# The first unit's product on split rows without the norm's factor, the factor applied to its results

## The chip, the cores and the metric

The kernel runs on one core of one Trainium2 chip. The metric is the device time of one execution in microseconds (us); a median over several executions is compared. Below, PE is the matrix engine, PEld its weight loads, DVE the vector engine, ACT the scalar engine, POOL the general engine and SP the engine whose queue issues most DMAs.

## What is computed

One layer of a decoder for 512 prompt tokens and 8 sample tokens, held together as 520 columns. Only the start of the layer matters here:

```python
h = rmsnorm(x, g_mix_pre)      # x * g * (1 / sqrt(mean(x*x) + eps)), per token
proj = h @ w_in                # 2048 -> q | k | v | B | C | u | gate_a | gate_b
...
merged = sigmoid(ga + b_gate[0]) * branch_a + sigmoid(gb + b_gate[1]) * branch_b
x = x + rmsnorm(merged @ w_o, g_mix_post)
# then the ConvFFN (up, causal conv, gelu, down) and the per-layer embedding
```

The norm's factor belongs to a token, that is, to a column of the kernel's matrices. So (x * g) @ w times the factor per column equals h @ w: the factor can be applied to the result.

## The kernel before

**Layout and units.** Activations lie feature-major: 16 rows of 128 features (k = 0 to 15) by 520 tokens, each token range cut into two halves of 260 (HALF). The weights come from memory as a stream of quarters `s_raw` (128x1024, four for each unit, two sets of buffers) which SP's queue loads. A unit produces two tiles of 128 output features for all tokens. Units 0 to 31 are the input projection; 0 and 1 are gates. Most units use a Strassen-like scheme of seven half-size products (j = 0 to 6) on sums and differences of weight quarters (`s1` to `s4`, on DVE) and of row blocks (`t1` to `t4`, on DVE, made once for all units of a set). A set's first unit is *plain* in three sets (`PLAIN`): all 16 rows times both tiles, without sums, so that the row blocks can be prepared meanwhile.

**Precision.** A product is either in fp32 (line 994 for the plain unit, line 1028 for the second unit, line 829 for k and v), or it is split: `v_hi`/`v_lo` are the high and low part of a weight tile, `o_hi`/`lo` those of a row block, and three cheaper fp32r matmuls (high by high, low by high, high by low) stand for one fp32 matmul (line 1063; line 1153 in the branches). High parts are ACT copies (`v_high`, `o_high`), low parts are DVE subtractions (`v_low`, `o_low`). `v_hi` and `v_lo` have four slots each.

**The start.** ACT scales each row of x into `raw4` (`x_tile`, line 1211) and squares it (1215), DVE adds the squares (1697), PE multiplies k's and v's weights with the rows that have no factor yet (829) and sums the squares over the features by `square_sum` (812). ACT takes the root (1195), DVE the reciprocal (1683), and `h_row` multiplies all 16 rows in place by the factor (1703). PE's plain unit 0 follows (994): 16 rows by two tiles by two halves, 64 fp32 matmuls, each shown in the trace as two records.

**Who waits for whom.** Every engine works through a queue written out in program order; semaphores join them. ACT copies the four results of unit 0 to `d_h` (`plain_unit`, line 1318, semaphores c11_out to c21_out) and the first three results of unit 1 (`copied`, line 1271: r1_out, r5_out, r2_out) so that PE may write their banks again: unit 1 begins after c11_out, its product j = 2 after r1_out, its product j = 4 after r2_out (`banks_free`). DVE's order is set by `plain_unit`, `second_unit` and `unit`. From unit 2 on PE needs `v_lo` and the low parts of the row blocks.

Of the kernel before, what the change touches and what calls it, by code (L numbers as in the profile page):

```python
# [90 lines left out]
def build(nc, sstream, x_in, p_in, chan_in, sinkp_in, sinks_in, cstate_in, fstate_in,  # L91
# [5 lines left out]
    with ExitStack() as ctx:  # L97
# [33 lines left out]
        x_raw = at("x_raw", [P, KD, T], r_op)  # L131

# [205 lines left out]
        SPLIT = split_of(range(U_O))  # L338
# [103 lines left out]
        x_rdy = sem("x_rdy")  # L442
        kv_used = sem("kv_used")
# [19 lines left out]
        ss_ready = sem("ss_ready")  # L463
        ss_scaled = sem("ss_scaled")
        ss_shift = sem("ss_shift")
        ss_exp = sem("ss_exp")
        ss_prob = sem("ss_prob")
        ss_turned = sem("ss_turned")
        ss_copied = sem("ss_copied")
        ss_out = sem("ss_out")  # L470
# [330 lines left out]
        def _(pe):  # L801
# [38 lines left out]
            def sample_scores():  # L840
# [4 lines left out]
                for g in range(NKV):  # L845
# [5 lines left out]
                    mm.then_inc(ss_ready, 1)  # L851

            def sample_turn():
                pe.wait_ge(ss_prob, 1)
# [3 lines left out]
                mm.then_inc(ss_turned, 1)  # L858

            def sample_values():  # L860
                pe.wait_ge(ss_copied, 1)
# [6 lines left out]
                mm.then_inc(ss_out, 1)  # L868
# [132 lines left out]

            def raw_product(s, u, j, parity):
# [7 lines left out]
                for h in range(2):  # L1010
# [117 lines left out]
            first_unit(0)  # L1128
# [57 lines left out]
        def _(act):  # L1186
# [1583 lines left out]
```

## Time and profile before

| | |
|---|---|
| median of 3 runs | 2680.53 us (2680.52 to 2681.27) |
| the profiled execution | 2679.39 us |
| its span in the profile | 2677.6 us |
| PE busy | 2663.8 us, 99% of the span |
| DVE busy | 2172.0 us, 81% |
| ACT busy | 1341.0 us, 50% |

The span is what the profile covers; the time of that execution is 1.8 us more. Times below count from the span's start. A busy share is an average over stages with different limits, so the start has to be read in its own rows.

### The profile page before, as it was taken

What the parts mean: (1) busy time and instruction counts of PE and PEld (TensorE: products, weight loads), DVE (VectorE), ACT (ScalarE), POOL (GpSimd) and SP (SyncE); (2) the same over time, 40 slices, a digit from 0 to 9 for tenths busy, and PEclk for the clock granted to TensorE, in tenths of its full rate; (3) what the DMA queues carried; (4) which work ended last, traced back from release to release, by engine and by line L of the source; (5) the groups of instructions that cost most, each with busy time, mean ns of one, the idle gap of its engine ahead of it and who ended that gap; (6) DMA issues with size and microseconds to landing.
All of it is one profiled execution on the core that took longest, in us unless ns stands there. A gap on an engine that the chain in (4) does not pass through costs nothing.

```text
span 2677.6 us, 54973 instructions
## 1 busy us (share of the span) xinstructions
PE 2663.8 (99%) x20917; PEld 2599.2 (97%) x20917; DVE 2172.0 (81%) x3809; ACT 1341.0 (50%) x2429; POOL 162.6 (6%) x251
## 2 busy tenths in 40 slices
PE   9999999999999999999999999999999999999999
PEld 8999999999999999989999999999999999999899
DVE  5998888888843687898888888888888768789987
ACT  5444555555532255645555555555555453445354
POOL 0110000000000000000000000000000000000000
PEclk9999999999999999999999999999999999999999
DMA  6443333333443355655566555665568575565684
GB/s 222 134 145 130 125 117 119 131 131 123 160 158 140 132 152 166 232 184 159 159 200 201 167 178 165 185 196 178 157 191 291 166 250 160 160 207 168 230 267 144
DMA packets 151348, 460.55 MB, mean 172 GB/s; under 512 B 16442, under 2 KB 46914, under 8 KB 147809
## 3 DMA queue, kind: packets, MB, share of 16 engines
q1 hardware_dynamic: 125040, 367.55, 38.8%
q0 software_dynamic: 26000, 90.86, 15.2%
q8 instruction: 80, 1.31, 0.2%
q14 instruction: 84, 0.68, 0.1%
q10 hardware_dynamic: 144, 0.15, 0.0%
HBM read 403.24 MB, written 54.11 MB: 171 GB/s over the span
## 4 chain that ended last, share of the span: by engine, by line
PE 98%; DVE 1%; issue 0%; ACT 0%; DVEq 0%; POOL 0%; ACTq 0%; POOLq 0%
PE pair L1063 77%; PE pair L1153 7%; PE pair L1028 7%; PE pair L994 3%; PE pair L829 1%; PE pair L1123 1%; PE pair L881 1%; PE pair L902 1%; DVE v_lo L1909 0%; PE pair L891 0%; PE pair L1180 0%; PE pair L960 0%; DVE lo L2007 0%; PE pair L818 0%; DVE lo_A L2007 0%
## 5 line engine op out<-in xcount | busy, mean ns | idle before, releaser
L1063 PE MATMUL pair<-o_hi,v_hi 128*128 128x260 f32 x5778 | 1638.0, 283 | 1.6 <-DVE f_low L2455 0.9
L1063 PE MATMUL pair<-o_hi,v_lo 128*128 128x260 f32 x5778 | 1631.4, 282 | 0.0
L1238 ACT ACTIVATE v_hi<-s_raw 128x512 fp32r<-128x512 f32 (+1 forms) x1328 | 828.9, 627 | 1007.3 <-PE pair L1063 810.5
L1063 PE MATMUL pair<-lo,v_hi 128*128 128x260 f32 x4140 | 1169.5, 282 | 0.0
L1909 DVE TENSOR_TENSOR v_lo<-s_raw,v_hi 128x512 fp32r<-128x512 f32 (+1 forms) x1264 | 859.2, 682 | 303.0 <-ACT v_hi L1238 267.1
L1063 PEld LDWEIGHTS pair<-o_hi,v_hi 128*128 128x128 f32 x5778 | 1086.4, 188 | 13.7 <-issue 12.0
L1063 PEld LDWEIGHTS pair<-o_hi,v_lo 128*128 128x128 f32 x5778 | 1088.2, 188 | 0.0
L1063 PEld LDWEIGHTS pair<-lo,v_hi 128*128 128x128 f32 x4140 | 778.1, 188 | 0.3
L1063 PE MATMUL pair<-lo_E,v_hi 128*128 128x260 f32 x834 | 236.0, 283 | 0.0
L1063 PE MATMUL pair<-lo_A,v_hi 128*128 128x260 f32 x804 | 226.7, 282 | 0.0
L1238 ACT ACTIVATE v_hi<-s_one 128x512 fp32r<-128x512 f32 (+1 forms) x212 | 132.2, 627 | 178.3 <-PE pair L1063 153.1
L1951 DVE TENSOR_TENSOR s_raw<-s_one,s_raw 128x512 f32<-128x512 f32 (+1 forms) x226 | 152.1, 676 | 15.4 <-PE pair L1028 15.4
L1063 PEld LDWEIGHTS pair<-lo_E,v_hi 128*128 128x128 f32 x834 | 156.4, 188 | 0.0
L1960 DVE TENSOR_TENSOR s_raw<-s_raw,s_raw 128x512 f32<-128x512 f32 (+1 forms) x226 | 152.3, 675 | 0.0
L1941 DVE TENSOR_TENSOR s_raw<-s_raw,s_raw 128x512 f32<-128x512 f32 (+1 forms) x226 | 151.3, 675 | 0.0
L1063 PEld LDWEIGHTS pair<-lo_A,v_hi 128*128 128x128 f32 x804 | 151.1, 188 | 0.0
L1909 DVE TENSOR_TENSOR v_lo<-s_one,v_hi 128x512 fp32r<-128x512 f32 (+1 forms) x212 | 143.4, 678 | 5.2 <-ACT v_hi L1238 1.5
L1028 PE MATMUL pair<-raw,s_raw 128*128 128x260 f32 x628 | 141.3, 383 | 2.7 <-DVE g_half L2185 1.7
L1028 PEld LDWEIGHTS pair<-raw,s_raw 128*128 128x128 f32 x628 | 118.4, 190 | 21.8 <-DVE g_half L2185 2.1
L2629 POOL DMA_DIRECT2D s_one<-in_sstream x81 | 44.5, 550 | 1377.0 <-DVE s_raw L1951 1042.2
L1153 PE MATMUL pair<-br_hi,v_lo 128*128 128x260 f32 x512 | 103.2, 283 | 0.0
L1153 PE MATMUL pair<-br_lo,v_hi 128*128 128x260 f32 x512 | 103.0, 283 | 0.0
(232 smaller groups left out, 2324.3 us busy)
## 6 DMA issues: line engine op xcount, KB each, us to landing
s_raw<-in_sstream SPq DMA_DIRECT2D x468, 512.0 KB, 4.6
s_one<-in_sstream POOLq DMA_DIRECT2D x146, 512.0 KB, 5.3
raw<-f_scr SPq DMA_DIRECT2D x12, 1040.0 KB, 7.1
s_raw<-in_sstream SPq DMA_DIRECT2D x32, 384.0 KB, 4.1
g_scr<-d_h SPq DMA_DIRECT2D x16, 520.0 KB, 2.7
g_in<-g_scr SPq DMA_DIRECT2D x32, 260.0 KB, 2.7
x_scr<-y_sb SPq DMA_DIRECT2D x8, 1040.0 KB, 5.1
s_one<-in_sstream POOLq DMA_DIRECT2D x16, 384.0 KB, 4.6
```

Of the source, the lines that this page charges most:

```text
L829: mm = pe.matmul(pair[2 + n][:, h, 0:HALF], w[:, quarter_of(k)[2]], x_half(k, h), start=k == 0, stop=k == KD - 1, skip_group_check=True)
L881: mm = pe.matmul(bank[g][:, v * 256 + key:(v + 1) * 256], q_blk[n % 2][HD * g:HD * g + HD, v, :], kT_sb[HD * g:HD * g + HD, blk * BLK + ke ...
L994: mm = pe.matmul(pair[a][:, b, 0:HALF], s_raw[r % 2][q][:, k % KH * P:(k % KH + 1) * P], src, start=k == 0, stop=k == nk * 2 - 1, skip_gro ...
L1028: mm = pe.matmul(out, w[:, kk * P:kk * P + P], src[:, k, :], start=j in (0, 1, 3) and k == 0, stop=k == nk - 1, skip_group_check=True)
L1063: mm = pe.matmul(out, wt[:, slot, kk * P:kk * P + P], r[:, k, :], start=j in (0, 1, 3) and k == 0 and n == 0, stop=k == nk - 1 and n == 2, ...
L1153: mm = pe.matmul(pair[2 + p][:, half, 0:HALF], wt[:, slot, kk * P:kk * P + P], r[:, half * HALF:(half + 1) * HALF], start=k == 0 and i == ...
L1238: nc.scalar.activation(v_hi[:, n % 4, 0:width], src, ACT.Copy, scale=0.5 if u == "br" else 1.0).then_inc(v_hi_rdy, 1)
L1909: ins = dve.tensor_tensor(v_lo[:, n % 4, 0:width], src, high, ALU.subtract)
L1941: dve.tensor_tensor(quarter(u, 2, h), quarter(u, 0, h), quarter(u, 2, h), ALU.subtract)\
L1951: dve.tensor_tensor(quarter(u, 0, h), w_src(u, 1, h), quarter(u, 0, h), ALU.subtract)\
L1960: dve.tensor_tensor(quarter(u, 1, h), quarter(u, 1, h), quarter(u, 0, h), ALU.subtract)\
L2629: pool.dma_start(s_one[:, 0:n], sstream[r_of(u), 2, :, 0:n]).then_inc(s1_dma, 16)
```

## The change

Unit 0 is no longer made in fp32. `split_plain_unit` (PE) multiplies high and low parts of the rows *without* the factor (`x_hi`, `x_lo`) with high and low parts of unit 0's weights: 192 fp32r matmuls in the place of 64 fp32 ones. ACT makes 16 `x_high` and 8 more `v_high`, DVE 16 `x_low` and 8 more `v_low`. The factor is multiplied into unit 0's two results `d_h` by DVE in unit 1 (`h_evac`, `g_first`). `h_row` stays, for all later units, and now waits for `x_lo` of its row. `square_sum` moves behind two more rows of k and v. Since `x_lo` and `x_hi` lie where the row blocks' parts will lie, `o_high` and `t2`, `t3`, `t4` wait for rows of unit 0 to be used; `t3` and `t4` move from ahead of unit 1 into it. Some semaphores of the sample's attention are merged. The first ACT table is that of Sqrt, and the load of it before the root goes.

```diff
+        x_lo = at("x_lo", [P, KD, T], r_op, f32r)
+        x_hi = at("x_hi", [P, KD, T], r_op + 4 * HB, f32r)
...
-        SPLIT = split_of(range(U_O))
+        SPLIT = [("first", i, 0) for i in range(8)] + split_of(range(U_O))
...
+        def rows_used(k):
+
+            return k - 1
...
+            if u == "first":
+                return rows_used(4 * (j // 2) + 3) - 1
...
+            if u == "first":
+                r, q = r_of(0), 2 * (j % 2) + j // 4
+                return r, q, s_raw[r % 2][q][:, (j // 2 % 2) * 4 * P:(j // 2 % 2 + 1) * 4 * P]
...
-                if k == KD - 4:
+                if k == KD - 2:
...
+            def split_plain_unit():
+
+                pe.wait_ge(root_rdy, 1)
+                for k in range(KD):
+                    if k % 4 == 0:
+                        pe.wait_ge(v_lo_rdy, k // 2 + 2)
+                    pe.wait_ge(x_lo_rdy, k + 1)
+                    for wt, r in ((v_hi, x_hi), (v_lo, x_hi), (v_hi, x_lo)):
+                        for n, outs in enumerate((((0, 1), (1, 1)), ((0, 0), (1, 0)))):
+                            slot = (k // 4 * 2 + n) % 4
+                            for h in range(2):
+                                a, b = outs[h]
+                                mm = pe.matmul(pair[a][:, b, 0:HALF],
+                                               wt[:, slot, k % 4 * P:k % 4 * P + P],
+                                               r[:, k, h * HALF:(h + 1) * HALF],
+                                               start=k == 0 and wt is v_hi and r is x_hi,
+                                               stop=k == KD - 1 and r is x_lo, skip_group_check=True)
+                    if k >= 2:
+                        mm.then_inc(v_used, 1)
+
...
+                    elif s == 0 and j in (0, 3, 5):
+                        pe.wait_ge(h_rdy, KD if j else KH)
...
-            first_unit(0)
+            split_plain_unit()
...
-            nc.scalar.activation(table_out[:, 6:7], ones[:, 0:1], ACT.Square)
+            nc.scalar.activation(table_out[:, 6:7], ones[:, 0:1], ACT.Sqrt)
+
+            def x_high(k):
+
+                act.wait_ge(x_rdy, k + 1)
+                nc.scalar.activation(x_hi[:, k, :].rearrange("p (h t) -> p h t", h=2), x_tile(k), ACT.Copy)\
+                  .then_inc(x_hi_rdy, 1)
...
+                    if 5 <= k < 13:
+                        x_high(k - 5)
+            v_high(0)
+            v_high(1)
             root(0)
+            for k in range(8, 12):
+                x_high(k)
+            v_high(2)
+            v_high(3)
+            for k in range(12, KD):
+                x_high(k)
             bias = chan[:, C_BGATE:C_BGATE + 2 * KD]
             nc.scalar.activation(bias, bias, ACT.Copy, scale=0.5).then_inc(bias_half, 1)
             warm(ACT.Exp, 1)
...
+                if s == 0 and j < 5:
+                    act.wait_ge(v_used, rows_used((3, 7, 11, 15, 3)[j]))
...
-                early = 1 if s == 2 else 5
+                early = {0: 3, 2: 1, S_GATE: 5}[s]
+                if s == 0:
+                    v_high(4)
+                    v_high(5)
                 for j in range(early):
                     o_high(s, j)
+                    if s == 0 and j == 0:
+                        v_high(6)
+                        v_high(7)
...
+                if u == 0:
+                    act.wait_ge(g_first, n + 1)
...
+            def x_low(k):
+
+                dve.wait_ge(x_hi_rdy, k + 1)
+                dve.wait_ge(sq_ready, k + 1)
+                dve.tensor_tensor(two(x_lo[:, k, :]), x_tile(k), two(x_hi[:, k, :].bitcast(f32)), ALU.subtract)\
+                   .then_inc(x_lo_rdy, 1)
...
+                if 6 <= k < 14:
+                    x_low(k - 6)
+            v_low(0)
+            v_low(1)
             invert(1)
...
+                dve.wait_ge(x_lo_rdy, k + 1)
...
+            def first_free(s, j):
+
+                if s == 0:
+                    dve.wait_ge(v_used, rows_used({2: 7, 4: 11, 6: 15}[j]))
+
...
-                if s in (0, 2):
+                if s == 2:
...
+                if s == 0:
+                    both_halves(s1, u + 1)
+                    both_halves(t2, s)
+                    both_halves(s3, u + 1)
+                    return
...
+                    if i == 1 and s == 0:
+                        both_halves(t3, s)
+                    if i == 4 and s == 0:
+                        both_halves(t4, s)
...
+                if u == 1 and i == 2:
+                    for n in range(2):
+                        for e in ((c11_out, c12_out), (c22_out, c21_out))[n]:
+                            dve.wait_ge(e, 1)
+                        dve.tensor_tensor(d_h[0][:, n, :], d_h[0][:, n, :], rstd[:, :], ALU.mult)\
+                           .then_inc(g_first, 1)
...
+            v_low(2)
+            v_low(3)
             st.wait()
-            for k in range(KD):
+            for k in range(KH):
+                h_row(k)
+            for k in range(KH, KH + 4):
+                x_low(k)
+            v_low(4)
+            v_low(5)
+            dve.wait_ge(h_rdy, KH)
+            both_halves(t1, 0)
+            for k in range(KH + 4, KD):
+                x_low(k)
+            v_low(6)
+            v_low(7)
+            for k in range(KH, KD):
                 h_row(k)
             dve.wait_ge(h_rdy, KD)
...
+            pool.wait_ge(g_first, 2)
```

**DVE from the reciprocal to t2.** `raw_60` is the rows, `s_one` and `s_raw` weights, `raw_E` what t2 makes. Before:

```order
L1683 RECIPROCAL rstd<-rstd 128x520 [waits root_rdy]
L1703 TENSOR_TENSOR raw_60<-raw_60,rstd 128x2x260 [waits kv_used,dve_step]
L1703 TENSOR_TENSOR raw_60<-raw_60,rstd 128x2x260 [waits kv_used] x15
L1933 TENSOR_TENSOR s_one<-s_raw_51,s_raw_52 128x512 [waits s_rdy03,s_rdy02,h_rdy]
L1933 TENSOR_TENSOR s_one<-s_raw_51,s_raw_52 128x512 [waits s_rdy03,s_rdy02]
L1941 TENSOR_TENSOR s_raw_51<-s_raw_49,s_raw_51 128x512 [waits s_rdy00] x2
L1971 TENSOR_TENSOR raw_60<-raw_60 128x1040 [waits v_used] x2
L1979 TENSOR_TENSOR raw_E<-raw_60 128x1040 [waits t1_done] x2
```

The same place in the changed kernel, right after the reciprocal, two `v_lo` and the first eight row multiplications:

```order
L1767 TENSOR_TENSOR x_lo<-raw_60,x_hi 128x520 [waits sq_ready,x_hi_rdy] x4
L1760 TENSOR_TENSOR v_lo<-s_raw_54,v_hi 128x512 [waits v_hi_rdy]
L1760 TENSOR_TENSOR v_lo<-s_raw_56,v_hi 128x512 [waits v_hi_rdy]
L2045 TENSOR_TENSOR raw_60<-raw_60 128x1040 [waits h_rdy]
L2045 TENSOR_TENSOR raw_60<-raw_60 128x1040
L1767 TENSOR_TENSOR x_lo<-raw_60,x_hi 128x520 [waits sq_ready,x_hi_rdy] x4
L1760 TENSOR_TENSOR v_lo<-s_raw_54,v_hi 128x512 [waits v_hi_rdy]
L1760 TENSOR_TENSOR v_lo<-s_raw_56,v_hi 128x512 [waits v_hi_rdy]
L1787 TENSOR_TENSOR raw_60<-raw_60,rstd 128x2x260 [waits kv_used,x_lo_rdy] x8
L2002 TENSOR_TENSOR s_one<-s_raw_51,s_raw_52 128x512 [waits s_rdy03,s_rdy02,h_rdy]
L2002 TENSOR_TENSOR s_one<-s_raw_51,s_raw_52 128x512 [waits s_rdy03,s_rdy02]
L2054 TENSOR_TENSOR raw_E<-raw_60 128x1040 [waits t1_done,v_used]
```

Eight `x_lo`, four `v_lo` and all sixteen row multiplications now stand ahead of `raw_E` (t2); t1 comes between them.

**DVE in unit 1.** `raw_79` is t3's block, `raw_80` t4's, the `lo` rows are the low parts for unit 2. Before, t3 and t4 precede the first row shown:

```order
L1951 TENSOR_TENSOR s_raw_49<-s_one,s_raw_49 128x512 [waits s1_done,v_used] x2
L2007 TENSOR_TENSOR lo_69<-raw_60,o_hi_62 128x1040 [waits o_hi_rdy,v_used] x2
L1933 TENSOR_TENSOR s_one<-s_raw_55,s_raw_56 128x512 [waits v_used,s2_done,s_rdy13,s_rdy12] x2
L2007 TENSOR_TENSOR lo_70<-raw_60,o_hi_63 128x1040 [waits o_hi_rdy,v_used] x2
L2007 TENSOR_TENSOR lo_E<-raw_E,o_hi_64 128x1040 [waits o_hi_rdy,v_used] x2
L1960 TENSOR_TENSOR s_raw_50<-s_raw_50,s_raw_49 128x512 [waits s2_done,v_used,s_rdy01]
```

In the changed kernel:

```order
L2020 TENSOR_TENSOR s_raw_49<-s_one,s_raw_49 128x512 [waits s1_done,v_used] x2
L2063 TENSOR_TENSOR raw_79<-raw_E,raw_60 128x1040 [waits t2_done,v_used]
L2063 TENSOR_TENSOR raw_79<-raw_E,raw_60 128x1040 [waits t2_done]
L2084 TENSOR_TENSOR lo_71<-raw_60,o_hi_64 128x1040 [waits o_hi_rdy,v_used] x2
L2347 TENSOR_TENSOR d_h_103<-d_h_103,rstd 128x520 [waits c12_out,c11_out]
L2347 TENSOR_TENSOR d_h_103<-d_h_103,rstd 128x520 [waits c21_out,c22_out]
L2002 TENSOR_TENSOR s_one<-s_raw_55,s_raw_56 128x512 [waits v_used,s2_done,s_rdy13,s_rdy12] x2
L2084 TENSOR_TENSOR lo_72<-raw_60,o_hi_65 128x1040 [waits o_hi_rdy,v_used] x2
L2071 TENSOR_TENSOR raw_80<-raw_60,raw_E 128x1040 [waits v_used]
L2071 TENSOR_TENSOR raw_80<-raw_60,raw_E 128x1040
L2084 TENSOR_TENSOR lo_E<-raw_E,o_hi_66 128x1040 [waits o_hi_rdy,v_used] x2
L2029 TENSOR_TENSOR s_raw_50<-s_raw_50,s_raw_49 128x512 [waits s2_done,v_used,s_rdy01]
```

t3, the two multiplications of `d_h` by `rstd`, and t4 have moved or come into the stretch that runs while PE makes unit 1.

**ACT around unit 0's results.** `o_hi_..` are the high parts of the row blocks, L1318 the four copies of unit 0's results, L1271 those of unit 1. Before:

```order
L1265 ACTIVATE o_hi_64<-raw_E 128x1040 [waits t2_done] x2
L1265 ACTIVATE o_hi_65<-raw_60 128x1040 [waits h_rdy] x2
L1265 ACTIVATE o_hi_66<-raw_77 128x1040 [waits t3_done] x2
L1318 ACTIVATE d_h_101<-pair 128x260 [waits v_used]
L1318 ACTIVATE d_h_101<-pair 128x260 x3
L1271 ACTIVATE d_h_102<-pair 128x260 [waits v_used]
L1265 ACTIVATE o_hi_67<-raw_60 128x1040 [waits h_rdy] x2
L1271 ACTIVATE d_h_102<-pair 128x260 [waits v_used]
L1265 ACTIVATE o_hi_68<-raw_78 128x1040 [waits t4_done] x2
L1271 ACTIVATE d_h_102<-pair 128x260 [waits v_used]
```

In the changed kernel these are L1314, L1373 and L1320:

```order
L1314 ACTIVATE o_hi_66<-raw_E 128x1040 [waits t2_done]
L1373 ACTIVATE d_h_103<-pair 128x260 [waits v_used]
L1373 ACTIVATE d_h_103<-pair 128x260 x3
L1314 ACTIVATE o_hi_67<-raw_60 128x1040 [waits h_rdy,v_used]
L1314 ACTIVATE o_hi_67<-raw_60 128x1040 [waits h_rdy]
L1314 ACTIVATE o_hi_68<-raw_79 128x1040 [waits t3_done,v_used]
L1314 ACTIVATE o_hi_68<-raw_79 128x1040 [waits t3_done]
L1320 ACTIVATE d_h_104<-pair 128x260 [waits v_used]
L1314 ACTIVATE o_hi_69<-raw_60 128x1040 [waits h_rdy] x2
L1320 ACTIVATE d_h_104<-pair 128x260 [waits v_used]
L1314 ACTIVATE o_hi_70<-raw_80 128x1040 [waits t4_done] x2
L1320 ACTIVATE d_h_104<-pair 128x260 [waits v_used]
```

The four copies still stand behind the high part of `raw_E`; the copy that is r1_out now stands behind the high parts of t3's block, and r2_out behind those of t4's block.

## Rows read from the trace of the kernel before

**Rows 1.** The page: busy time, share of the span, instructions; the chain.

```profile
PE 2663.8 (99%) x20917; PEld 2599.2 (97%) x20917; DVE 2172.0 (81%) x3809; ACT 1341.0 (50%) x2429; POOL 162.6 (6%) x251
...
PE 98%; DVE 1%; issue 0%; ACT 0%; DVEq 0%; POOL 0%; ACTq 0%; POOLq 0%
```

**Rows 2.** Timeline of PE: start us, duration us, engine, line, names, count.

```profile
0.99 4.21 PE L818 MATMUL pair<-ones 128*128 128x128 f32 x18 [0.99 <-POOL table_out L2560]
5.12 22.22 PE L829 MATMUL pair<-raw,s_raw 128*128 128x260 f32 x96
27.18 1.04 PE L812 MATMUL pair<-sqacc,ones 128*128 128x260 f32 x4
28.05 7.18 PE L829 MATMUL pair<-raw,s_raw 128*128 128x260 f32 x32
35.07 28.22 PE L994 MATMUL pair<-raw,s_raw 128*128 128x260 f32 x128
```

**Rows 3.** Timeline of PE, units 1 and 2.

```profile
63.76 3.77 PE L1028 MATMUL pair<-raw,s_raw 128*128 128x260 f32 x16 [0.48 <-ACT d_h L1318]
...
88.22 0.47 PE L1063 MATMUL pair<-o_hi,v_hi 128*128 128x260 f32 x1
```

**Rows 4.** One line's records: duration min/median/max ns, first and last start.

```profile
L1153 PE MATMUL pair<-br_hi,v_hi x512: 278/282/288, 743.1 to 927.0; 128*128 128x260 f32 x171
...
L1153 PE MATMUL pair<-br_hi,v_lo x512: 277/283/291, 743.6 to 927.5; 128*128 128x260 f32 x171
```

**Rows 5.** Who PE waited for, whole span: us in total, times, longest.

```profile
PE pair L1028 <- DVE g_half L2185: 1.7, 1, 1.7
...
PE pair L1028 <- ACT d_h L1318: 0.5, 1, 0.5
```

**Rows 6.** Timeline of ACT.

```profile
24.27 0.64 ACT L1215 ACTIVATE sq_a<-x_raw 128x520 f32<-128x520 f32 x1
...
28.25 0.69 ACT L1195 ACTIVATE rstd<-pair,table_out 128x520 f32<-128x520 f32 x1 [1.83 <-PE pair L812]
...
51.72 2.22 ACT L1265 ACTIVATE o_hi<-raw_E 128x1040 fp32r<-128x1040 f32 x2
...
63.32 1.23 ACT L1318 ACTIVATE d_h<-pair 128x260 f32<-128x260 f32 x4 [5.53 <-PE pair L994]
...
71.08 0.39 ACT L1271 ACTIVATE d_h<-pair 128x260 f32<-128x260 f32 x1 [1.20 <-PE pair L1028]
```

**Rows 7.** Timeline of ACT, weights of unit 2.

```profile
76.11 1.14 ACT L1238 ACTIVATE v_hi<-s_raw 128x512 fp32r<-128x512 f32 x2
```

**Rows 8.** Timeline of DVE.

```profile
28.98 3.40 DVE L1683 RECIPROCAL rstd<-rstd 128x520 f32<-128x520 f32 x1 [3.34 <-ACT rstd L1195]
32.42 9.86 DVE L1703 TENSOR_TENSOR raw<-raw,rstd 128x520 f32<-128x520 f32 x16
42.31 1.29 DVE L1933 TENSOR_TENSOR s_one<-s_raw,s_raw 128x512 f32<-128x512 f32 x2
...
50.45 2.39 DVE L1979 TENSOR_TENSOR raw_E<-raw 128x1040 f32<-128x1040 f32 x2
...
65.82 0.69 DVE L1951 TENSOR_TENSOR s_raw<-s_one,s_raw 128x512 f32<-128x512 f32 x1 [8.37 <-PE pair L1028]
```

**Rows 9.** Timeline of DVE, unit 1.

```profile
74.16 2.38 DVE L2007 TENSOR_TENSOR lo_E<-raw_E,o_hi 128x1040 fp32r<-128x1040 f32 x2
...
78.09 0.43 DVE L2181 TENSOR_TENSOR d_h<-pair,d_h 128x260 f32<-128x260 f32 x1 [0.94 <-PE pair L1028]
...
88.43 0.68 DVE L1909 TENSOR_TENSOR v_lo<-s_raw,v_hi 128x512 fp32r<-128x512 f32 x1
```

**Rows 10.** Groups of PE in 7.5 to 9.2 us: count, busy us, mean ns.

```profile
L829 PE MATMUL pair<-raw,s_raw 128*128 128x260 f32 x9 | 2.1, 383 | 0.0
```

**Rows 11.** Groups of PE in 5 to 6.2 us.

```profile
L829 PE MATMUL pair<-raw,s_raw 128*128 128x260 f32 x3 | 1.7, 695 | 0.0
```

**Rows 12.** Records of line 1028: duration min/median/max ns.

```profile
L1028 PE MATMUL pair<-raw,s_raw x628: 380/382/487, 63.8 to 2550.3; 128*128 128x260 f32 x157
```

More of the change, by code:

```diff
@@ L442, in build @@
         x_rdy = sem("x_rdy")
+        x_hi_rdy = sem("x_hi_rdy")
+        x_lo_rdy = sem("x_lo_rdy")
+        g_first = sem("g_first")
         kv_used = sem("kv_used")
@@ L462, in build @@
         kc_in = sem("kc_in")
[L463 to L470, printed above, removed]
+        sample_pe = sem("sample_pe")
+        sample_act = sem("sample_act")
+        sample_dve = sem("sample_dve")
         as_rdy = sem("as_rdy")
@@ L1202, in half_root, with v_high @@
                                      scale=1.0 / D, bias=eps).then_inc(root_rdy, 1)
+            def v_high(n):
+                if n >= len(SPLIT):
+                    return
+                if n >= 4:
+                    act.wait_ge(v_used, used_by(n - 4) + 1)
+                u, j, h = SPLIT[n]
+                r, q, src = split_src(n)
+                if j == 1 and u not in ("first", "br", "ple"):
+                    sum_ready_1(act, u, h)
+                elif q is None:
+                    act.wait_ge({2: s2_done, 4: s3_done, 5: s4_done}[j], 2 * (u - earlier(u)) + h + 1)
+                else:
+                    act.wait_ge(s_rdy[r % 2][q], 16 * (r // 2 + 1))
+                width = src.shape[1]
+                nc.scalar.activation(v_hi[:, n % 4, 0:width], src, ACT.Copy,
+                                     scale=0.5 if u == "br" else 1.0).then_inc(v_hi_rdy, 1)
             act.dma_start(chan[:, :], chan_in).then_inc(chan_ready, 16)
             act.wait_ge(pool_set, 1)
-            nc.scalar.activation(table_out[:, 6:7], ones[:, 0:1], ACT.Square)
+            nc.scalar.activation(table_out[:, 6:7], ones[:, 0:1], ACT.Sqrt)
[3 more added lines that the diff above has]
+                  .then_inc(x_hi_rdy, 1)
             act.wait_ge(chan_ready, 16)
@@ L1689, in half_invert, with v_low @@
                 st.done(dve.reciprocal(half, half))
+            def v_low(n):
+                if n >= len(SPLIT):
+                    return
+                dve.wait_ge(v_hi_rdy, n + 1)
+                src = split_src(n)[2]
+                width = src.shape[1]
+                high = v_hi[:, n % 4, 0:width].bitcast(f32)
+                if SPLIT[n][0] == "br":
+                    ins = dve.scalar_tensor_tensor(out=v_lo[:, n % 4, 0:width], in0=src, scalar=0.5,
+                                                   in1=high, op0=ALU.mult, op1=ALU.subtract)
+                else:
+                    ins = dve.tensor_tensor(v_lo[:, n % 4, 0:width], src, high, ALU.subtract)
+                ins.then_inc(v_lo_rdy, 1)
+            def x_low(k):
[3 more added lines that the diff above has]
+                   .then_inc(x_lo_rdy, 1)
             for k in range(1, KD):
@@ L1975, in t2 @@
                 if h == 0:
+                    first_free(s, 2)
                     slot_free(dve, s, 2)
```

72 lines of the change are left out of this document (23 added, 49 removed).

## The prediction

> **What bounds the kernel now.** I read the page first: PE is busy 99% of the span and carries 98% of the chain [rows 1]. So PE time that goes is a gain, unless a wait takes its place, and DVE's and ACT's work counts only where PE waits for it. Then PE's own waits: nearly none, and at the start one of 0.5 us, for ACT's copy of unit 0's first result [rows 5]. Then the three timelines of the start. PE runs k and v with the square sum until 35.07, unit 0 from there for 28.22, unit 1 from 63.76, unit 2 from 88.22 [rows 2, 3]. The reader should see in DVE's timeline that the reciprocal ends at 32.38, that row multiplications and sums follow without a gap, and that DVE later idles for 8.37 before 65.82 [rows 8]: unit 0's 28 us are long enough to prepare everything for unit 1. In unit 1 DVE has almost no rest: from 74.16 to 89.11, when the second `v_lo` of unit 2 is done, it idles 0.94 [rows 9]. PE wants that `v_lo` one half product after 88.22, at 89.66. The slack there is 0.55.
>
> **Unit 0 on PE.** 28.22 for 64 fp32 products go [rows 2], 192 fp32r matmuls of 260 columns come. Their pace stands in line 1153, which also uses each weight for two halves in turn: 1536 of them start from 743.1 to 927.5, 0.120 each [rows 4]. 192 times 0.120 is 23.0. As bounds I take 0.110 (a quarter of 28.22/64 = 0.441, if an fp32 product is four passes) and 0.124 (PEld's busy time over its instructions, 2599.2/20917 [rows 1]), 21.1 to 23.8 for the unit. With 0.120, the pace of the same pattern, unit 0 runs from 35.07 to 58.1 and ends 5.2 earlier than now. By the Trainium skill, "TensorE: Matmul & The Clock Gate", section "Back-to-back issue gap", a matmul of 260 columns takes 260/2.4 + 2.5 = 111 ns: an estimate of 21.3 for the unit. The trace has 120 and decides. By the page's figure the sum at the end would be the same, since PE would only wait 1.7 longer for the next step.
>
> **DVE up to unit 1's release.** The square sum moves behind 8 more fp32 matmuls. Sixteen take 28.05 to 35.07, so this is 3.5 [rows 2]; root and reciprocal move with it, and the reciprocal ends at 35.9 instead of 32.4. Are the squares in time for 27.18 + 3.5 = 30.7? ACT's last square ended at 24.91 [rows 6]; eight `x_high` at 0.54 (a pair of the like `v_hi` takes 1.14 with some overlap [rows 7]) make it 29.2, DVE's add 29.9. Cover 0.8; if it went, each us would come on top of all below. The first eight `x_low` and two `v_low` fit in the time before the root.
> From 35.9 to t2's end DVE does, back to back: 16 row multiplications 9.8 (9.86 for 16, 0.61 each [rows 8]), eight `x_low` at the same 0.61, 4.9; six `v_low` at 0.60 (two weight sums take 1.29 [rows 8]), 3.6; t1 2.3, two sums for unit 1 1.2, t2 2.4 (2.39 for a pair [rows 8]). Sum 24.2: t2 ends at 60.1. Before it ended at 52.84, 10 us ahead of unit 0's end. ACT's queue has the high part of t2's block ahead of the four copies of unit 0's results. It ended 1.1 after t2 (53.94 to 52.84 [rows 6, 8]), so now at about 61.1, and PE starts 0.44 after the copies begin (63.76 to 63.32 [rows 3, 6]). Unit 1 starts at 61.5. PE waits 3.4 there instead of 0.5, and of the 5.2 only 2.3 are left. `x_low` is not in the trace: its nearest rows are DVE's 520-wide ones at 0.61; as bounds I take 0.54 (ACT's like copy) and 0.69 (no overlap between neighbours, a single row's 0.69 [rows 8]), which moves t2 by -0.6 or +0.7.
>
> **Unit 1.** A product takes 3.5 ((88.22 - 63.76)/7 [rows 3]). Where t3 and t4 were done before unit 1, they now come inside.
> - r1_out: t3 stands behind s2, which waits for product 0's end, 65.15. s2's second half ends the wait at 65.75, t3 takes until 68.1, its high part on ACT until 69.1, and only then comes the copy of product 0 (0.39 [rows 6]). PE wants its bank at 61.5 + 7.0 = 68.5 and gets it at 69.5: 1.0.
> - r2_out: DVE goes on with a low part 2.3, the two new multiplications by the factor 1.2, two sums 1.2, a low part 2.3, and t4 2.4: 77.4. High part and copy: 78.9. PE wants it at 69.5 + 7.0 = 76.5: 2.4.
> - `v_lo` of unit 2: behind t4 DVE's order is the old one from 74.16 to 89.11, 14.0 without its idle 0.94 [rows 9]. Started at 77.35 it ends at 91.4. PE has unit 2's first half done at 78.9 + 10.5 + 1.44 = 90.8 (12 matmuls at 0.120 are 1.44): 0.6.
> The new multiplications have no other price: the sigmoids and the rope behind them have a unit of time. The saved load of ACT's root table lay in an idle stretch, nothing. The merged semaphores: nothing. Loads of unit 2's weights are issued earlier, nothing waits for them.
>
> **Sum.** -5.2 + 2.9 + 1.0 + 2.4 + 0.6 = +1.7: at 91.4 PE stands where it stood at 89.66. From there both programs are the same and PE never idles long enough to give it back. 2679.39 of the profiled execution become 2681.1. That execution lies 1.14 below the median of 2680.53, so the median should become 2682.2.
>
> **Rivals.**
> - *The gain arrives.* If DVE and ACT kept up, PE would keep 5.2: 2675.3. For it: PE is 99% busy. Against: 24.2 us of DVE work between 35.9 and t2's end against 23.0 of PE. Chance 0.06.
> - *Part of it arrives.* t2 and its high part come in time for 58.1 (DVE pieces cheaper than their nearest rows), the waits inside unit 1 stay: +1.7 - 2.9 = -1.2, 2679.3. It needs 3 us less in 24. Chance 0.10.
> - *Slower: the clock.* This is the case on the other side. PE would idle 3.4 in one piece after 58.1. The longest idle of the trace is 1.7 [rows 5], and line 1028, where it lies, never had a record over 487 ns, median 382 [rows 12]: that idle left the clock at its upper level. After a start from rest it is otherwise: nine 128-column products took 4.1, 0.46 each, as long as 260 columns later [rows 2], and line 829's records are 695 ns on average at 5 to 6.2 but 383 at 7.5 to 9.2 [rows 10, 11]. So from rest PE ran at 1.2 GHz for about 5.6 us (0.99 to 6.6), though the page's clock row prints no fall, and half of that, 2.8, is lost. After the idle before unit 1 this would cost 2.8 more: +4.5, 2685.0. It decides for slower by over 0.2% only if the low level holds for over 7.4 us (5.4 less 1.7, times two). The Trainium skill, same page, section "Part 1: The HAM clock gate", says that a PE that has been idle falls back to 1.2 GHz. By that rule the case happens if this idle is long enough, which no row of this trace shows, and the time would be the 2685.0 above. Chance 0.12, of which 0.04 beyond 0.2%.
> - *PE starves inside unit 0.* It needs the `v_lo` of rows 8 and 12 at 46.6 and 52.3; by the sum they are done at 45.6 and 51.6, 0.7 to 1.0 ahead. With `x_low` at 0.9 each t2 comes 2.4 later: +4.1, 2684.6. No row speaks for such a price. Chance 0.04.
> The forecast has 0.68.
>
> **Numbers.** Predicted 2682.2. The likeliest case's own range is 2681.4 to 2683.1 (`x_low`'s two bounds, and some tenths of run to run: three runs spread over 0.75). The clock case and the partial gain belong in the range: 2679.3 to 2685.2, which leaves out the full gain and the tails of the slow cases. 0.2% is 5.4 us, about what a measurement of this kernel can tell from no change. Even the full gain is less than that. Faster 0.02, same 0.93, slower 0.05.
>
> **What would show it.** In the changed profile: the split unit from 35.1 to 58.1 without a gap and at 0.12 a matmul; PE's waits on ACT's d_h of 3.4, 1.0 and 2.4 and on DVE's v_lo of 0.6; DVE without idle from 35.9 to 61; the reciprocal at 32.4. I would be wrong if the first record of line 1060 started before 60, if records of it stood at twice 382 ns, or if unit 2 began before 88.2.

## The result, and the profile after

| | before | changed |
|---|---|---|
| median | 2680.15 us (18 runs, 2678.62 to 2681.94) | 2685.69 us (18 runs, 2683.47 to 2688.56) |
| profiled execution: time, span | 2679.39, 2677.6 us | 2686.37, 2684.6 us |

The changed kernel is slower by 5.5 us: ratio 1.0020, 95% interval 1.0014 to 1.0026. The prediction was 2682.2, a loss of 1.7, with a range that ended at 2685.2; its case "slower: the clock" was 2685.0. The time is half a microsecond outside the range. One execution of the runs below, of e3, took 3727.70 us at a mean granted clock of 0.654 and is left out of e3's figures.

The page: busy time and the chain, as [rows 1].

```profile
PE 2663.3 (99%) x20981; PEld 2600.2 (97%) x20981; DVE 2187.5 (81%) x3835; ACT 1350.2 (50%) x2451; POOL 162.6 (6%) x251
...
PE 94%; DVE 4%; issue 1%; DMA 1%; ACT 0%; DVEq 0%; ACTq 0%; POOL 0%; POOLq 0%
```

PE is busy for 0.5 us less than before. Its share of the chain fell from 98% to 94%; DVE has 4% instead of 1%. The new unit on PE, by its line's records (duration min/median/max ns, first and last start):

```profile
L1024 PE MATMUL pair<-x_hi,v_hi x64: 277/282/472, 34.7 to 56.7; 128*128 128x260 f32 x64
...
L1024 PE MATMUL pair<-x_lo,v_hi x64: 278/282/288, 35.9 to 57.7; 128*128 128x260 f32 x64
```

It runs from 34.7 to 58.0, 0.120 us a matmul, without a wait: the 5.2 us are won. Then PE's timeline to unit 2, as [rows 3]:

```profile
61.30 5.44 PE L1060 MATMUL pair<-raw,s_raw 128*128 128x260 f32 x16 [3.33 <-ACT d_h L1373]
66.58 3.67 PE L1060 MATMUL pair<-raw,s_one 128*128 128x260 f32 x16
71.21 3.77 PE L1060 MATMUL pair<-raw_E,s_raw 128*128 128x260 f32 x16 [0.96 <-ACT d_h L1320]
74.82 3.67 PE L1060 MATMUL pair<-raw,s_raw 128*128 128x260 f32 x16
80.55 12.47 PE L1060 MATMUL pair<-raw,s_raw 128*128 128x260 f32 x48 [2.06 <-ACT d_h L1320]
...
92.67 0.47 PE L1095 MATMUL pair<-o_hi,v_hi 128*128 128x260 f32 x1
```

Three waits in brackets: 3.3, 1.0, 2.1. And two durations that no wait explains: the first product took 5.44 where its neighbours take 3.7, the last three 12.47 where three like the others would take 10.8. Each is 1.7 too long. The prediction's sign, records of this line at twice 382 ns, is there (duration min/median/max ns):

```profile
L1060 PE MATMUL pair<-raw,s_raw x80: 382/383/802, 61.3 to 92.6; 128*128 128x260 f32 x80
```

Unit 2 begins at 92.67, 4.45 later than in [rows 3]. The same stretch in windows (us, PE busy and matmuls, granted clock as a share of 2.4 GHz, DMA share, GB/s):

```profile
58.00:61.00 3.00, 0.00 (x0) 1.00 0.67 176
61.00:65.00 4.00, 3.70 (x9) 0.57 0.32 130
65.00:81.00 16.00, 12.98 (x58) 1.00 0.01 1
81.00:82.00 1.00, 1.00 (x6) 0.89 0.00 0
82.00:85.00 3.00, 3.00 (x8) 0.50 0.44 178
85.00:92.00 7.00, 7.00 (x33) 0.99 0.45 128
```

The granted clock fell to 1.2 GHz twice, for 3.4 us each time: the first time as PE began again after 3.3 us of idle, the second a microsecond behind the wait of 2.1. In windows of 1 us nothing between lies under 0.99. 3.4 us at half rate are the 1.7 us that the durations show.

PE's waits, as [rows 5]; below them the timelines of DVE and ACT, as [rows 8] and [rows 6]:

```profile
PE pair L1060 <- ACT d_h L1373: 3.3, 1, 3.3
PE pair L1060 <- ACT d_h L1320: 3.0, 2, 2.1
...
PE pair L1095 <- DVE v_lo L1760: 1.5, 3, 0.8
...
PE pair L1095 <- DVE d_h L2271: 0.7, 2, 0.5
```

None of the 1.5 us for `v_lo` lies where the prediction put 0.6, in unit 2's first products: 0.8 is behind 180 us, and the other two, 0.2 and 0.5, are in the kernel before as well. A second profile of the changed kernel, with one fall of the clock instead of two, has 0.33 there:

```profile
93.03 0.36 PE L1095 MATMUL pair<-o_hi,v_hi 128*128 128x260 f32 x1 [0.33 <-DVE v_lo L1760]
```

DVE, then ACT:

```profile
32.33 3.41 DVE L1740 RECIPROCAL rstd<-rstd 128x520 f32<-128x520 f32 x1 [1.41 <-ACT rstd L1227]
...
36.78 4.97 DVE L1787 TENSOR_TENSOR raw<-raw,rstd 128x520 f32<-128x520 f32 x8
41.67 2.53 DVE L1767 TENSOR_TENSOR x_lo<-raw,x_hi 128x520 fp32r<-128x520 f32 x4
...
57.48 2.39 DVE L2054 TENSOR_TENSOR raw_E<-raw 128x1040 f32<-128x1040 f32 x2
59.78 1.29 DVE L2010 TENSOR_TENSOR s_raw<-s_raw,s_raw 128x512 f32<-128x512 f32 x2
```

```profile
58.81 2.16 ACT L1314 ACTIVATE o_hi<-raw_E 128x1040 fp32r<-128x1040 f32 x2 [9.15 <-DVE raw_E L2054]
60.88 1.20 ACT L1373 ACTIVATE d_h<-pair 128x260 f32<-128x260 f32 x4
```

DVE runs on from the reciprocal to 61 without a gap, `x_lo` costs 0.61 each, t2 ends at 59.87. ACT, idle for 9.15 us, makes t2's high part first and the four copies behind it; PE has nothing to do from 58.0 to 61.3.

### The profile page after: what moved, and what is told of

It is laid out like the page before. It is cut to its first block, busy times and chain, and to the rows that moved or that the text cites. A ratio compares the mean times of both kernels' runs of the same rounds, so it can differ in the third digit from the quotient of the medians.

```text
span 2684.6 us, 55205 instructions
## 1 busy us (share of the span) xinstructions
PE 2663.3 (99%) x20981; PEld 2600.2 (97%) x20981; DVE 2187.5 (81%) x3835; ACT 1350.2 (50%) x2451; POOL 162.6 (6%) x251
## 4 chain that ended last, share of the span: by engine, by line
PE 94%; DVE 4%; issue 1%; DMA 1%; ACT 0%; DVEq 0%; ACTq 0%; POOL 0%; POOLq 0%
PE pair L1095 74%; PE pair L1185 7%; PE pair L1060 6%; PE pair L1004 2%; DVE v_lo L1760 1%; PE pair L839 1%; PE pair L1155 1%; PE pair L891 1%; PE pair L912 1%; DMA rope_s<-d_h 0%; DMA s_one<-in_sstream 0%; DVE raw L1787 0%; PE pair L901 0%; DVE lo L2084 0%; DVE s_raw L2029 0%
```

## Experiments

Theory: the queues of DVE and ACT cost what the prediction summed (+1.7 net), and the clock takes the rest. Rival: a wait costs its own length and no more, and the rest comes from transfers behind unit 2. In the table the loss is the median less that of the kernel before on the same chip; "stretches" are those at 0.50 in the one profiled execution; the last column counts the executions whose mean granted clock prints as 1.000. The medians are of 11 executions (10 for e3) against 33 of the kernel before (15 for e10). "Filled" means that useless matmuls stand where PE would wait.

| run | loss, us | ratio, 95% interval | stretches | at 1.000 |
|---|---|---|---|---|
| changed, again | +6.1 | 1.0020 (1.0011 to 1.0029) | one | 0 of 11 |
| e1 all waits filled | +1.6 | 1.0007 (0.9998 to 1.0016) | none | 5 of 11 |
| e6 filled ahead of unit 1 | +2.4 | 1.0008 (0.9999 to 1.0017) | none | 7 of 11 |
| e7 filled inside unit 1 | +3.7 | 1.0013 (1.0004 to 1.0022) | one | 0 of 11 |
| e2 copies first | +1.0 | 1.0004 (0.9995 to 1.0013) | one | 5 of 11 |
| e3 before, table loads | +4.4 | 1.0016 (1.0007 to 1.0026) | one, of 6.8 us | 1 of 10 |
| e3b the same, filled | +4.6 | 1.0017 (1.0008 to 1.0026) | none | 10 of 11 |
| e5 before, held | +5.4 | 1.0019 (1.0010 to 1.0028) | one | 0 of 11 |
| e5b the same, filled | +4.1 | 1.0015 (1.0006 to 1.0024) | none | 7 of 11 |
| e9 before, held short | +3.3 | 1.0011 (1.0002 to 1.0020) | none | 4 of 11 |
| e4b copies, filled | -0.8 | 0.9995 (0.9986 to 1.0004) | none | 7 of 11 |
| e8 factor on GpSimd | -0.2 | 1.0000 (0.9991 to 1.0009) | none | 3 of 11 |
| e10 copies, filled, low parts later | -1.3 | 0.9995 (0.9986 to 1.0004) | none | 6 of 11 |

The last column says something of every execution, not only of the profiled one. A stretch of 3.4 us at half clock takes 1.7 us off some 2680, 0.06%, so an execution that prints 1.000 holds none. The reverse doesn't follow: in the profiles the clock is also at 0.50 for the last 0.6 to 3.4 us of the span, and of 114 executions of the kernel before 74 print 1.000, 40 print 0.999 and none 0.998. Of the 30 of the changed kernel none prints 1.000, and 14 print 0.998, which takes at least 4.0 us off: more than one stretch and the end together ((3.4 + 3.4)/2 = 3.4). So all 30 can have had the first fall, and at least 14, about half, had two.

**e1: PE kept at work in the waits.**

```diff
+            def filler(n):
+                for _ in range(n):
+                    pe.matmul(pair[2][:, 0, 384:512], ones[:, :], ones[:, :], start=True, stop=True,
+                              skip_group_check=True)
...
+                if isinstance(u, int) and u == 1:
+                    filler({0: 14, 2: 4, 4: 9}.get(j, 0))
                 banks_free(s, u, j, parity)
```

> The changed kernel with 14, 4 and 9 matmuls without use (ones by ones, 128 columns, into a free part of a bank) ahead of unit 1's products 0, 2 and 4, where PE waits; nothing else is changed. Clock theory (the two stretches of 3.4 us at 1.2 GHz behind these waits cost up to 1.7 us each): the waits end at the same times, the low stretches go, and the kernel is 1.7 us slower than before, 3.4 to 3.8 faster than the changed kernel. Rival (the missing 3.8 us come from DVE's work or late DMAs further on, the clock is an accident of the profile): still 5 to 5.5 slower than before.

Measured +1.6. PE's timeline of e1 (L1035 is the filler, L1068 unit 1):

```profile
58.09 3.29 PE L1035 MATMUL pair<-ones 128*128 128x128 f32 x28
61.62 3.77 PE L1068 MATMUL pair<-raw,s_raw 128*128 128x260 f32 x16 [0.24 <-ACT d_h L1381]
...
76.97 2.17 PE L1035 MATMUL pair<-ones 128*128 128x128 f32 x18
79.19 10.79 PE L1068 MATMUL pair<-raw,s_raw 128*128 128x260 f32 x48
```

Unit 1 begins when it did (0.3 later, as unit 0 did), and its products take 3.77 and 10.79: the operands were as late as ever, and only the clock was kept up. Work that computes nothing made the changed kernel some 4 us faster.

**e6 and e7: one wait or the other.** The counts in e1's edit are `{0: 14}` in e6 and `{2: 4, 4: 9}` in e7.

> The changed kernel with 14 products of ones with ones (results unused) only in the wait of 3.3 us ahead of unit 1; the waits in unit 1 stay bare. Clock theory: the stretch at 0.50 at the start of unit 1, worth 1.7 us, is gone in every run and the one behind the waits of 1.0 and 2.1 us in unit 1 stays possible: +2 to +4 us against the kernel before, 1.7 to 3 below the changed kernel. Rival (nothing but the waits' own length and transfers behind unit 2): +5.5 us, as the changed kernel.

> The changed kernel with 4 and 9 such products only in the two waits inside unit 1 (1.0 and 2.1 us), and the wait of 3.3 us ahead of it bare. Clock theory: one stretch at 0.50, at the start of unit 1, in nearly every run: 1.7 (queues) + 1.7 (one stretch of 3.4 us at half rate) = +3.4 us or a little more. Rival: +5.5 us.

> The changed kernel again, unchanged, beside the others. Both theories: +5.5 us against the kernel before, as in the result; the wait ahead of unit 1 about 3.3 us. Clock theory: its profile shows one or two stretches of 3.4 us at a granted clock of 0.50 between the end of unit 0 and the middle of unit 1. Rival (the remainder of +3.8 us beyond the queues comes from transfers behind unit 2): no such stretch is needed, and the waits of VectorE for the rope rows sum to 5 us again against 2.3 before.

Measured +2.4, +3.7, and +6.1 for the changed kernel (on another chip). e7 keeps the first stretch and costs 2.1 more than e1; e6 costs 0.9 more than e1, less than a stretch: its profile has the bare wait of 2.06 and no fall behind it. The second fall comes in some executions only: it is in two of three profiles of the changed kernel, the first fall in all three. The mean clocks agree: 7 of e6's 11 executions print 1.000, so they had no fall; none of e7's does. The rival's +5.5 lies outside the intervals of e1 and e6, which end at 4.3 and 4.6 us, and inside that of e7, whose case rests on its profile and its clocks.

**e2: the copies ahead of t2's high part.** `early = {0: 3, ...}` becomes `{0: 2, ...}`, so that ACT copies unit 0's results before the third high part.

> The changed kernel with ACT's copies of unit 0's results ahead of the high part of t2's block (2 blocks ahead of the copies instead of 3). Queue theory: the wait ahead of unit 1 falls from 3.3 to about 0.6, unit 1 starts at 58.6 instead of 61.3, the waits of 1.0 and 2.1 inside unit 1 stay, and so does one of 0.5 for v_lo. Without any clock loss 1.2 faster than before; with one low stretch behind the 2.1 wait about 0.5 slower than before. Rival (DVE alone sets the start of unit 2, whatever ACT's order): no gain over the changed kernel, 5.5 slower than before.

Measured +1.0. PE's timeline of e2:

```profile
58.58 3.77 PE L1060 MATMUL pair<-raw,s_raw 128*128 128x260 f32 x16 [0.48 <-ACT d_h L1373]
...
76.16 12.47 PE L1060 MATMUL pair<-raw,s_raw 128*128 128x260 f32 x48 [2.05 <-ACT d_h L1320]
```

The wait of 3.3 is gone, as t2's data are not needed by unit 1's first product; the fall behind the wait of 2.05 stayed in this execution. The five executions that print 1.000 have a median of 2679.53, the six others 2681.05: 1.5 more, near the 1.7 of a fall. Even without a fall nothing is left of the 1.2 expected; where it went was not looked for.

**e3, e3b, e5, e5b, e9: an idle of PE in the kernel before.** These add no part of the change. e3 lets ACT load its tables again ahead of the copies; e5 holds the copies until DVE has made four small reciprocals; e9 takes two; the b kernels add 14 fillers ahead of unit 1. In e5, e5b and e9 the first two reciprocals (the first pair of tiles) write over the last 4 of the 260 columns of `pair[3]`. These are results of v's product (line 829 with n = 1), not of unit 0 as e9's expectation says, and DVE reads them later (`kv_evac`). So these three kernels give wrong values for a few tokens; the order of work and the shapes stay.

```diff
                 act.wait_ge(v_used, h_of(u, 6, 1) + 1)
+                if s == 0:
+                    warm(ACT.Exp, 2)
+                    warm(ACT.Sqrt, 3)
+                    warm(ACT.Exp, 4)
```

That is e3; e5 and e9 have, with 4 and 2 reciprocals:

```diff
+                if s == 0:
+                    act.wait_ge(held, 1)
...
+                    dve.wait_ge(v_used, 14)
+                    for n in range(4):
+                        ins = dve.reciprocal(pair[3][:, n % 2, 256 + n // 2 * 128:384 + n // 2 * 128], ones[:, :])
+                    ins.then_inc(held, 1)
```

> The kernel before, with two loads of ACT tables and three one-column activations between the end of unit 0 and its copies: PE waits about 3.6 us ahead of unit 1 instead of 0.5, all else is as before. Clock theory: 3.1 for the wait and up to 1.7 for a low stretch of 3.4 us behind it: 3.1 to 4.8 slower than before. Rival (an idle of 3.6 costs only itself): 3.1 slower.

> As the one before, with 14 matmuls without use in the wait: 3.1 slower than before by both theories, and no stretch at 1.2 GHz at this place. The difference to the kernel without them is the price of the clock alone.

> The kernel before, with its unit 1 held back: once TensorE has done unit 0, VectorE computes four reciprocals of a 128x128 tile of ones, and only then may ScalarE copy unit 0's results out; no other work is added. TensorE then waits some 4 us ahead of unit 1 where it waited 0.5. By the queues alone the kernel gets +4.0 us. Clock theory: an idle of that length costs the clock as well, 3.4 to 7 us at 0.50 behind it, so +7 to +8 us, with products of unit 1 at twice their time. Rival (a wait costs its own length and no more): +4.0 us.

> The same held kernel, with 14 products of ones with ones (results unused) on TensorE in the wait ahead of unit 1. By the queues +4.0 us, as they end before the operands come. Clock theory: +4.0 us, no product of unit 1 slower than 3.8 us, and about 3 us less than without them. Rival: +4.0 us, the same as without them.

> The kernel before, held as in the held kernel but with two reciprocals in place of four (their first tile overwrites the last 4 of 260 columns of unit 0's results in one bank pair): TensorE waits some 2.3 us ahead of unit 1 where it waited 0.5, so +1.8 us by the wait's own length. Clock theory with a gap of this length enough: +3.5 us and a stretch of 3.4 us at 0.50. Clock theory with this gap too short: +1.8 us, no such stretch. Rival (a wait costs its own length): +1.8 us.

Unit 1's first product in e3, in e5, in e5b and in e9, a fence each:

```profile
66.42 6.83 PE L1028 MATMUL pair<-raw,s_raw 128*128 128x260 f32 x16 [3.57 <-ACT d_h L1322]
```

```profile
66.68 5.46 PE L1029 MATMUL pair<-raw,s_raw 128*128 128x260 f32 x16 [3.97 <-ACT d_h L1321]
```

```profile
67.53 3.77 PE L1037 MATMUL pair<-raw,s_raw 128*128 128x260 f32 x16 [0.84 <-ACT d_h L1329]
```

```profile
65.48 3.77 PE L1029 MATMUL pair<-raw,s_raw 128*128 128x260 f32 x16 [2.34 <-ACT d_h L1321]
```

In e5 PE waits 3.97 instead of 0.48, 3.5 more, and the product takes 1.7 longer: 5.2, measured 5.4. Filled, the product takes 3.77 again; e5b costs 1.3 less than e5, though 0.6 more than the 3.5 of its wait. So an idle of that length brings the fall in a kernel without the change: it needs the idle, not the new matmuls. By their intervals alone e5 and e5b are not told apart (2.7 to 7.5 and 1.6 to 6.4 us); the profiles tell them, and the clocks: none of e5's 11 executions prints 1.000, 7 of e5b's do. I had put the hold at 4.0; it was 3.5, and the loss expected for e5 by the clock (7 to 8) reckoned with up to two such stretches.

e3's profile shows it too, for 6.8 us at 0.50. But its filled twin was no faster over its runs (+4.6 where +3.1 was expected, against e3's +4.4), although its own profiled execution, the lowest of the eleven, began unit 1 at full clock, and 10 of the eleven print 1.000 where 1 of e3's ten does. So in this pair the fillers did keep the clock up and no time was won. This speaks against a fixed price of 1.7 us for a fall; what costs e3b the 1.5 us is open, and it is why e5 was made. The one execution of e3 that prints 1.000 had no such stretch: an idle of this length, if it had the same, need not bring the fall.

e9's profiled execution has no fall after 2.34 and is 1.9 above before's median, as its own length says. It is the second lowest of eleven; nine lie between 2682.8 and 2684.6, where a fall would put them. But two of the nine (2683.49 and 2683.95) print 1.000 and had none; whether the other seven had one is not shown, and e3b and e5b, with 1.5 and 0.6 us above their waits and no fall, show that a loss of this size has other causes too.

**The stretch behind unit 2.** The point of comparison is DVE's copy of unit 2's last result; here before, changed, and before in another execution:

```profile
133.16 0.42 DVE L2313 COPY d_h<-pair 128x260 f32<-128x260 f32 x1
```

```profile
137.60 0.42 DVE L2405 COPY d_h<-pair 128x260 f32<-128x260 f32 x1
```

```profile
132.85 0.42 DVE L2313 COPY d_h<-pair 128x260 f32<-128x260 f32 x1
```

At 133 us the changed kernel is 4.4 behind, at the end of the span 7.0. Between them DVE waits for the turned rows of the query. Before, first profile:

```profile
155.59 0.70 DVE L1729 TENSOR_TENSOR rope_s<-rope_s,sin 128x520 f32<-128x520 f32 x1 [0.78 <-DMA rope_s<-d_h]
...
176.52 0.70 DVE L1729 TENSOR_TENSOR rope_s<-rope_s,sin 128x520 f32<-128x520 f32 x1 [1.54 <-DMA rope_s<-d_h]
```

The changed kernel:

```profile
161.07 0.70 DVE L1813 TENSOR_TENSOR rope_s<-rope_s,sin 128x520 f32<-128x520 f32 x1 [1.80 <-DMA rope_s<-d_h]
...
183.05 0.70 DVE L1813 TENSOR_TENSOR rope_s<-rope_s,sin 128x520 f32<-128x520 f32 x1 [3.15 <-DMA rope_s<-d_h]
```

So three single executions were profiled, of the kernel before twice and of the changed one:

> The kernel before, unchanged, in another execution. If the loss between 152 and 190 us is a matter of the execution (how the turned rows' transfers fall against the loads of weights), its two waits of VectorE there differ from the 0.8 and 1.5 us of the first profile, by up to a microsecond or more. If it comes from the change, they are 0.8 and 1.5 us again, within 0.2.

> As the run beside it: the kernel before once more. Two waits of VectorE for the turned rows between 152 and 190 us: other than 0.8 and 1.5 us if they belong to the execution, the same if they belong to the kernel.

> The changed kernel once more. By the queues and the clock it stands 3.3 us (one stretch at 0.50) or 4.4 to 5 us (two) behind the kernel before at 140 us. Waits of VectorE for the turned rows between 152 and 190 us: 1.8 and 3.2 us again if the change causes them, anything from 0.8 to 3 if they belong to the execution.

They took 2680.36, 2680.09 and 2684.73 us. The kernel before, first of the two:

```profile
156.16 0.70 DVE L1729 TENSOR_TENSOR rope_s<-rope_s,sin 128x520 f32<-128x520 f32 x1 [1.64 <-DMA rope_s<-d_h]
...
177.44 0.70 DVE L1729 TENSOR_TENSOR rope_s<-rope_s,sin 128x520 f32<-128x520 f32 x1 [2.45 <-DMA rope_s<-d_h]
```

The other has 1.44 and 2.53; the changed kernel has 1.79 and 1.79 here and 2.42 and 1.33 in the profile of its repetition. These waits belong to the execution: before's first profile had a lucky one, and the rival's evidence was that. Over three profiles of each kernel the spans differ by 5.1 (2683.3 and 2678.1), of which 4.2 stand at 133 us; the 0.9 behind it is inside what one kernel's executions differ by there (1.2), and three of each can't call it zero.

**e4b, e8, e10: can the gain be had?** ACT's order: copies first, the third and fourth high parts behind them and each later one behind one more copy of unit 1's results. e4b and e10 have fillers in the waits that are left: 2, 6 and 2 ahead of unit 1's products 0, 5 and 6, and e4b 7 more ahead of unit 2. That is 17 and 10, not the 23 and 16 of the expectations.

```diff
-                early = {0: 3, 2: 1, S_GATE: 5}[s]
+                early = {0: 2, 2: 1, S_GATE: 5}[s]
...
-                for j in range(early, 2 if s == 2 else 5):
+                for j in range(early, {0: 4, 2: 2, S_GATE: 5}[s]):
...
+                    elif s == 0:
+                        if i in (1, 3, 5):
+                            o_high(s, 4 + i // 2)
...
```

e8 and e10 also move DVE's (VectorE's) low parts, and e8, without fillers, makes the two multiplications by the factor on POOL (GpSimd, `pool`) and not on DVE:

```diff
+                if s == 0:
+                    lows = {1: 0, 3: 1, 5: 2, 7: 3, 12: 4, 13: 5}
...
+                pool.tensor_tensor(d_h[0][:, n, :], d_h[0][:, n, :], rstd[:, :], ALU.mult)\
+                    .then_inc(g_first, 1)
```

> The changed kernel with ScalarE's order about unit 1 changed (the copy of unit 0's results goes ahead of the third, fourth and later high parts of unit 1's operand, each of which moves behind one more copy) and 23 products of ones with ones in four waits of TensorE (2 ahead of unit 1, 6 and 6 and 2 in it, 7 ahead of unit 2). By the queues alone TensorE's waits ahead of and in unit 1 shrink to 1.4, 0.7 and 1.8 us, and 1.2 us of unit 0's 5.2 us arrive at the end: -1.2 us against the kernel before. Clock theory: -1.2 us. Rival (the remainder comes from transfers behind unit 2): -1.2 + 3.8 = +2.6 us, as that is not touched here.

> The changed kernel, with the multiplication of unit 0's results by the norm's factor on GpSimd, which has no work there, ScalarE's copies of unit 0's results ahead of the third high part as in the two kernels with the copies first, and VectorE's fifth and sixth low parts behind the low parts of unit 2's first weights; no filler. Theory (VectorE's queue through unit 1 is what holds the gain back, as it is busy from 72 to 92 us): the waits in unit 1 fall to 0.2 and 0.7 us and the one behind it to about 1.4, so -2.8 us against the kernel before by the queues, with no stretch at 0.50. Rival (GpSimd is slow at this or holds VectorE up while it runs, so that nothing is won by it): -1.2 to 0 us, as with the copies first.

> The changed kernel with ScalarE's copies first and the 16 products of ones ahead of and in unit 1, as in the run with the copies first and the fillers, and with VectorE's fifth and sixth low parts behind the low parts of unit 2's first weights; the factor stays on VectorE. By the queues 0.4 us better than that run: -1.6 us at 140 us in the profile, and -1.2 us by the median, as that run's was 0.4 short of its sum. Rival (the low parts' order changes nothing, as the wait only moves from ahead of unit 2 into it): -0.8 us, as that run.

Measured -0.8, -0.2 and -1.3. e4b and e10 follow the queues within 0.4. Neither is told from the kernel before by its interval; e10 has the lowest median of all, and its median is nearly 7 us under that of the changed kernel (5.5 and 1.3, each against the kernel before on its chip). In e8 GpSimd's two multiplications and DVE's work beside them were

```profile
58.77 3.92 POOL L2669 TENSOR_TENSOR d_h<-d_h,rstd 128x520 f32<-128x520 f32 x2 [57.51 <-ACT d_h L1373]
```

```profile
59.75 3.49 DVE L2011 TENSOR_TENSOR s_raw<-s_raw,s_raw 128x512 f32<-128x512 f32 x2
```

The two sums of weights took 3.49 where the changed kernel's take 1.29 (1.28 in e2 and 1.29 in e10, which also copy first). Taking 1.3 us of work from DVE cost it 2.2: the rival to e8 was right. PE's waits in unit 1 were 1.7 and 0.4 and the one behind it 1.2, where 0.2, 0.7 and 1.4 were expected. By the Trainium skill, "SBUF — State Buffer", section "Who interferes with whom", a VectorE operation with two SBUF inputs and a GpSimd operation that reads SBUF contend for a shared pair of ports that only one of them holds at a time. The trace agrees that DVE is held, for 2.2 us beside GpSimd's 3.92: its second sum ended 0.55 after GpSimd's last multiplication (63.24 and 62.69), about the 0.6 that one such sum takes.

## Why the prediction was wrong

- **Unit 0 on PE**: right. 0.120 a matmul, 34.7 to 58.0 for 35.1 to 58.1; the -5.2 holds. The Trainium skill's 111 ns ("TensorE: Matmul & The Clock Gate", section "Back-to-back issue gap", which gives the formula for the isolated gap) is not what this pattern does: the trace has 120.
- **DVE up to unit 1**: right to 0.3. Reciprocal at its end 35.74 (35.9), `x_lo` 0.61 each, t2 done at 59.87 (60.1), wait 3.33 (3.4).
- **Waits in unit 1**: right within 0.4. 0.96 and 2.06 for 1.0 and 2.4. For the 0.6 of `v_lo` in unit 2, e1 and the second profile of the changed kernel have 0.33, and the profiles with two falls nothing, as PE came later. The whole queue sum, +1.7, agrees with e1's +1.6 (interval -0.5 to +4.3).
- **The step that failed** is the sum's missing term for the clock: the forecast put the price of an idle of 3.4 us beyond its own length at nothing, and was held at 0.68 against 0.12 for "slower: the clock". The runs showed one or two stretches of 3.4 us at half clock in its place, 1.7 us of matmul time each. The argument was that 1.7 us of idle had left the clock up [rows 5, 12]; it bounded the effect from one side only and said nothing of 3.4. The three profiles of the changed kernel and e7's show the fall at unit 1, e1's and e6's that it goes when the idle is filled, and e5 that it comes after such an idle without the change. By the Trainium skill, same page, section "Part 1: The HAM clock gate", a PE that has been idle falls back to 1.2 GHz; the trace of the changed kernel agrees, with 0.50 granted from 61.3 to 64.7, behind 3.3 us of idle.
- **Its size** was off as well. I priced one fall, at 2.8, from the start of the program, where the matmuls ran at half rate for 5.6 us (the granted clock of both traces reads 1.00 there). A fall in the middle of the program held for 3.4 us and costs 1.7. But about half of the executions had two, the second behind the waits of 1.0 and 2.1 in unit 1, and a second was not thought of. So the queues and the clock give 1.7 + 1.7 = 3.4 or 1.7 + 3.4 = 5.1; 5.5 was measured, and 6.1 in the repetition. What lies over, 0.4 to 2.7 us, is not attributed; the three profiles of each kernel leave 0.9 behind unit 2, inside the scatter there. That the clock case's 2685.0 came close to 2685.7 is luck: one stretch priced too high stood for one or two and a rest.
- The bound "over 0.2% only if the low level holds for over 7.4 us" did not quite hold: the loss is 0.207% with at most 6.8 us at the low level in a profile, because of that rest.

## What to carry to other kernels

When a faster stage leaves the matmul engine waiting for several microseconds, add a term for the clock to the wait (here 1.7 us, half of a stretch of 3.4, for each fall), and don't take a shorter idle that did no harm as proof. First shorten the gap by order (what the next product doesn't need goes behind what it needs), and where a gap stays, try useless matmuls that end before the operands come: they kept the clock up in every profile here and won some 4 us in e1, 1.3 in e5b and nothing in e3b. A gain on a 99% busy engine arrives only so far as the queues that feed it have slack: here 24 us of VectorE work stood against 23 us of matmuls, 3 of the 5 us won were gone before unit 1 began, and by unit 2 the queues had cost all 5 and 1.7 more, before the clock's share.

## What the runs showed of the hardware that I had not expected

- The low level held for 3.4 us in the changed kernel, e2, e5 and e7 and for 6.8 us in e3. It followed all six bare idles of 3.3 to 4.0 us that were profiled (one execution of e3 that was not profiled had no such stretch, by its mean clock), three of five pairs of 1.0 and 2.1, not the one of 2.34 in e9, and none of 1.7.
- The fall need not come where the wait is. In the changed kernel's first profile PE ran at full clock for a microsecond behind the wait of 2.06 and then at half; behind that of 3.33 it was low with the first matmul, and in the second profile behind the same wait a microsecond later. During the idle itself the granted clock reads 1.00 (58 to 61 us).
- A two-input operation of GpSimd in SBUF (1.96 us for 128x520 f32) slowed DVE's beside it from 0.65 to 1.75 us each.
